# A hybrid encoder layer: tokens transposed before they are modulated

## What is computed

```
mod = silu(c) @ ada_w + ada_b                      # six rows of 1024 per group
sh1, sc1, g1, sh2, sc2, g2 = split(mod, 6)
h = rms_norm(x, norm1_g) * (1 + sc1) + sh1
z = h @ w_in                                       # q, k, v and the inputs of the recurrence
x = x + g1 * (concat[attention(q,k,v), rwkv7(z)] @ w_out)
h = rms_norm(x, norm2_g) * (1 + sc2) + sh2
x = x + g2 * experts(h)                            # top-1 group, top-2 experts
y = rms_norm(x, final_g)
```

## Time and profile before

| | |
|---|---|
| time, median of 3 runs | 1817.06 us (1814.21 to 1818.36) |
| the profiled execution | 1818.64 us, span 1816.9 us |
| PE busy | 1437.8 us (79%) |
| DVE, ACT, POOL busy | 623.9, 464.4, 297.5 us |
| moved | 321.22 MB, mean 177 GB/s |

### The profile page before, as it was taken

The page is one execution under the profiler, slowest core; times in us unless marked ns, Lnnn a source line. Parts: engine busy times, 40 slices in busy tenths (PEclk is TensorE's granted clock), DMA queues, the critical chain, the costliest instruction groups (busy, mean ns, idle before and its releaser), DMA issues. The chain is left out here.

```text
span 1816.9 us, 22753 instructions
## 1 busy us (share of the span) xinstructions
PE 1437.8 (79%) x8896; PEld 878.3 (48%) x8896; DVE 623.9 (34%) x1044; ACT 464.4 (26%) x1072; POOL 297.5 (16%) x278
## 2 busy tenths in 40 slices
PE   5799999996629999999989689719877777777750
PEld 1445456654217777777767335405443434343420
DVE  0500044331756666666667632320000000000006
ACT  1201124432224455544546211101100000000003
POOL 0000023220562222122230510030000000000002
PEclk9799999998759999999999789759989998989995
DMA  6535441111341000100000372169999999999975
GB/s 226 180 121 186 152 138 47 47 36 50 112 167 36 19 19 22 33 18 19 19 1 2 109 261 85 69 245 371 376 380 376 386 378 386 378 385 377 385 284 194
DMA packets 161374, 321.22 MB, mean 177 GB/s; under 512 B 12544, under 2 KB 37248, under 8 KB 160908
## 3 DMA queue, kind: packets, MB, share of 16 engines
q1 hardware_dynamic: 150636, 295.42, 45.6%
q0 software_dynamic: 4672, 14.69, 2.7%
q10 hardware_dynamic: 5984, 9.97, 1.5%
HBM read 288.05 MB, written 32.00 MB: 176 GB/s over the span
## 5 line engine op out<-in xcount | busy, mean ns | idle before, releaser
L1207 PE MATMUL bank<-arena 128*128 128x128 f16 (+6 forms) x3696 | 434.7, 272 | 68.4 <-DMA arena<-direction_scratch 29.8
L1207 PEld LDWEIGHTS bank<-arena 128*128 128x128 f16 (+1 forms) x3696 | 336.6, 138 | 164.9 <-issue 99.0
L1857 PE MATMUL bank<-arena 128*64 128x256 f32 x2048 | 268.1, 422 | 100.6 <-DMA arena<-in_exp_w 63.8
L1857 PEld LDWEIGHTS bank<-arena 128*64 128x64 f32 x2048 | 165.9, 152 | 214.4 <-issue 88.4
L610 PE MATMUL bank<-arena 128*128 128x512 f32 x368 | 167.0, 601 | 0.7 <-ACT arena L359 0.7
L1043 ACT CAST arena<-bank 128x384 f16<-128x384 f32 x360 | 158.5, 482 | 15.9 <-PE bank L1207 11.1
L1823 DVE TENSOR_TENSOR arena<-bank,arena 128x256 f32<-128x256 f32 x32 | 13.6, 426 | 374.1 <-PE bank L1857 374.1
L1163 DVE CAST arena<-bank 128x384 f16<-128x384 f32 x216 | 116.8, 556 | 64.6 <-PE bank L1207 62.9
L1875 PE MATMUL bank<-arena 128*64 128x512 f32 x512 | 116.9, 598 | 19.1 <-ACT arena L1796 19.1
L347 POOL TENSOR_SCALAR arena<-arena 128x256 f32<-128x256 f32 (+1 forms) x64 | 51.9, 821 | 354.2 <-DVE arena L538 354.2
L610 PEld LDWEIGHTS bank<-arena 128*128 128x128 f32 x368 | 66.8, 189 | 85.2 <-issue 83.3
(11 more groups left out here) (238 smaller groups left out, 1422.6 us busy)
## 6 DMA issues: line engine op xcount, KB each, us to landing
arena<-in_exp_w SPq DMA_DIRECT2D x96, 2048.0 KB, 21.0
arena<-in_ada_w SPq DMA_DIRECT2D x12, 2048.0 KB
arena<-in_w_in SPq DMA_DIRECT2D x23, 512.0 KB, 4.3
direction_scratch<-arena SPq DMA_DIRECT2D x6, 1536.0 KB, 5.5
arena<-direction_scratch SPq DMA_DIRECT2D x12, 768.0 KB, 4.6
slot_out<-arena ACTq DMA_DIRECT2D x64, 128.0 KB, 5.7
slot_out<-arena SPq DMA_DIRECT2D x1, 6144.0 KB
arena<-in_x_sample SPq DMA_DIRECT2D x8, 512.0 KB, 4.8
```

The lines of the kernel that those rows point to most:

```text
L1207: return nc.tensor.matmul(out, lhsT, r, start=start, stop=True, skip_group_check=True)
L1857: ins = nc.tensor.matmul(bank[b + 2 * c.s][BLK * n:BLK * n + BLK, 0:HALF], xT[c.s][:, j, :], slot[c.w][:, j, n * HALF:(n + 1) * HALF], sta ...
```

## The change

Tiles of x are only normalised (one DVE product with the reciprocal root) before they are transposed. Shift and scale are not spread over partitions; instead `mod_columns` turns each chunk of modp into columns, one value per feature on the partition of that feature, by four small matmuls, and DVE copies them to mcol. Then each transposed block is scaled and shifted in place with per-partition scalars, blocks 0, 1, 4, 5 by DVE and 2, 3, 6, 7 by ACT. Chunks come in the order 2, 3, 0, 1 (scale first). PE interleaves the transposes of the tiles with the chunks. The transposes alternate between two pairs of PSUM banks, x has four buffers. The first loads are x(0), identity, eps and x(1), ahead of the first chunk; the gain comes as a column, not broadcast; ada_b for the first four chunks comes in one load. project(0) comes ahead of the values. Cut to its core:

```diff
+        n1c = take(KD)
+        mcol = take(4 * KD).rearrange("p (m k g) -> p m k g", m=2, g=2)
...
+        NXB = 4
...
-        xb = [take(D) for _ in range(2)]
+        xb = [take(D) for _ in range(NXB)]
         hb = [take(D) for _ in range(2)]
-        rows = take(4 * D).rearrange("p (g m d) -> p g m d", g=2, m=2)
-        n1_row = take(D)
+        assert top[0] <= base5 + P // 2 + 5 * W + 3 * NT * W
+        adab4 = catT[:, 0:4, :].rearrange("p c t -> p (c t)")[:, 0:4 * 512]
...
-        ring = [("ada", c) for c in range(WV)] + [("wv", 0)] + [("ada", c) for c in range(WV, NCHUNK)]
+        ring = [("ada", c) for c in (2, 3, 0, 1)] + [("wv", 0)] + [("ada", c) for c in range(WV, NCHUNK)]
...
-            early = [(sel, A["c_sel"]), (ident, A["c_ident"]), (eps, A["c_eps"]), (mu[:, :, 0:2], A["mu"]),
-                     (n1_row, A["norm1_g"][0].partition_broadcast(P))]
...
             def x(t):
-                if t >= 2:
-                    sp.wait_ge(sem("x_used"), t - 1)
-                sp.dma_start(xb[t % 2], x_tile[t]).then_inc(sem(f"x_in{t % 2}"), 16)
+                if t >= NXB:
+                    sp.wait_ge(sem("x_used"), t - NXB + 1)
+                sp.dma_start(xb[t % NXB], x_tile[t]).then_inc(sem(f"x_in{t % NXB}"), 16)
+            x(0)
+            sp.dma_start(ident, A["c_ident"]).then_inc(sem("consts_in"), 16)
+            sp.dma_start(eps, A["c_eps"]).then_inc(sem("consts_in"), 16)
+            x(1)
             wide(0)
-            for dst, src in early:
-                sp.dma_start(dst, src).then_inc(sem("consts_in"), 16)
-            x(0)
-            x(1)
...
-                wide(r)
-            for t in range(2, NT):
-                x(t)
+            sp.dma_start(sel, A["c_sel"]).then_inc(sem("sel_in"), 16)
+            sp.dma_start(adab4[0:1, :], A["ada_b"][0:1, 0:4 * 512]).then_inc(sem("sel_in"), 16)
+            sp.dma_start(n1c, A["n1_cols"]).then_inc(sem("cols_in"), 16)
+            sp.dma_start(mu[:, :, 0:2], A["mu"]).then_inc(sem("cols_in"), 16)
+            x(2)
+            x(3)
+            wide(1)
+            x(4)
+            x(5)
+            wide(2)
+            win(0)
+            wide(3)
             wide(4)
-            for i in range(NWIN):
+            for i in range(1, NWIN):
...
                 act.wait_ge(sem("mod_mm"), i + 1)
-                nc.scalar.copy(modp[:, i * 512:(i + 1) * 512], bank[i % 2]).then_inc(sem("mod_ready"), 1)
-            for i in range(4):
-                mod(i)
+                c = i if i >= WV else ring[i][1]
+                nc.scalar.copy(modp[:, c * 512:(c + 1) * 512], bank[i % 2]).then_inc(sem("mod_ready"), 1)
...
             def rms(t):
-                act.wait_ge(sem(f"x_in{t % 2}"), 16 * (t // 2 + 1))
+                act.wait_ge(sem(f"x_in{t % NXB}"), 16 * (t // NXB + 1))
                 if t:
                     own.wait(own.n)
-                own.link(nc.scalar.activation(sq1, xb[t % 2], ACT.Square, scale=1.0 / 32.0, accum_out=stat[:, t, 0:1]))
+                own.link(nc.scalar.activation(sq1, xb[t % NXB], ACT.Square, scale=1.0 / 32.0, accum_out=stat[:, t, 0:1]))
                 own.done(nc.scalar.activation(stat[:, t, 1:2], stat[:, t, 0:1], ACT.Sqrt, bias=eps[:, 0:1]))
...
+            def hT_evac(t):
+                act.wait_ge(sem("hT_mm"), 2 * t + 1)
+                nc.scalar.copy(hT_half[0][:, :, t * P:(t + 1) * P], bank[2 + 2 * (t % 2)].rearrange("p (k c) -> p k c", k=4)).then_inc(sem("hT_act"), 1)
+            def modulate(k):
+                act.wait_ge(sem("cols_ready"), k // 4 + 3)
+                for g, (lo, hi) in enumerate(((0, T_S), (T_S, TOK))):
+                    nc.scalar.activation(hTk[k][:, lo:hi], hTk[k][:, lo:hi], ACT.Identity, bias=mcol[:, 0, k, g:g + 1],
+                                         scale=mcol[:, 1, k, g:g + 1]).then_inc(sem("h_act"), 1)
             rms(0)
...
-                act.dma_start(v_dram[t * P:(t + 1) * P, :], zs[t % 2][:, 0:W]).then_inc(sem(f"v_out{t % 2}"), 16)
+            hT_evac(0)
+            rms(2)
+            hT_evac(1)
+            rms(3)
+            mod(0)
+            hT_evac(2)
+            rms(4)
+            hT_evac(3)
+            rms(5)
+            mod(1)
+            hT_evac(4)
+            hT_evac(5)
+            mod(2)
+            act.wait_ge(sem("hT_act"), NT)
+            act.wait_ge(sem("hT_dve"), NT)
+            modulate(2)
+            modulate(3)
+            mod(3)
+            modulate(6)
+            modulate(7)
+            def values_out():
+                for t in range(NT):
+                    act.wait_ge(sem("v_mm"), t + 1)
+                    if t >= 2:
+                        act.wait_ge(sem(f"v_out{t % 2}"), 16 * (t // 2))
+                    nc.scalar.copy(zs[t % 2][:, 0:W], bank[2 + t % 2]).then_inc(sem("v_ready"), 1)
+                    act.wait_ge(sem("v_ready"), t + 1)
...
+                if i == 0:
+                    values_out()
...
-                ins = nc.vector.scalar_tensor_tensor(hb[t % 2], xb[t % 2], stat[:, t, 2:3], rows[:, group(t), 1, :], ALU.mult, ALU.mult)
-                ins.then_inc(sem("x_used"), 1)
-                dve.wait_ge(sem("x_used"), t + 1)
-                nc.vector.tensor_tensor(hb[t % 2], hb[t % 2], rows[:, group(t), 0, :], ALU.add).then_inc(sem("h_ready"), 1)
+                nc.vector.tensor_scalar(hb[t % 2], xb[t % NXB], stat[:, t, 2:3], None, ALU.mult).then_inc(sem("x_used"), 1)
...
+            def columns(r):
+                ks = slice(4 * (r % 2), 4 * (r % 2) + 4)
+                src = bank[6 + r % 2][:, 0:8].rearrange("p (k g) -> p k g", g=2)
+                dve.wait_ge(sem("cols_mm"), r + 1)
+                if r < 2:
+                    ins = nc.vector.scalar_tensor_tensor(mcol[:, 1, ks, :], src, 1.0, n1c[:, ks].unsqueeze(2).to_broadcast([P, 4, 2]), ALU.add, ALU.mult)
+                else:
+                    ins = nc.vector.tensor_copy(mcol[:, 0, ks, :], src)
+                ins.then_inc(sem("cols_ready"), 1)
+            def modulate(k):
+                for g, (lo, hi) in enumerate(((0, T_S), (T_S, TOK))):
+                    nc.vector.tensor_scalar(hTk[k][:, lo:hi], hTk[k][:, lo:hi], mcol[:, 1, k, g:g + 1], mcol[:, 0, k, g:g + 1],
+                                            ALU.mult, ALU.add).then_inc(sem("h_dve"), 1)
+            columns(0)
+            columns(1)
+            columns(2)
+            dve.wait_ge(sem("hT_act"), NT)
+            dve.wait_ge(sem("hT_dve"), NT)
+            dve.wait_ge(sem("cols_ready"), 3)
+            modulate(0)
+            modulate(1)
+            columns(3)
+            dve.wait_ge(sem("cols_ready"), 4)
+            modulate(4)
+            modulate(5)
...
+            def first_mod(r):
+                if r >= 2:
+                    pe.wait_ge(sem("mod_ready"), r - 1)
+                c = ring[r][1]
+                nc.tensor.matmul(bank[r % 2][0:32, :], sel[0:1, 2, 0:32], adab4[0:1, c * 512:(c + 1) * 512], start=True, stop=False)
+                pe.wait_ge(sem(f"wide_in{r % 2}"), 32 * (r // 2 + 1))
+                for k in range(2):
+                    for q in range(4):
+                        ins = nc.tensor.matmul(bank[r % 2][32 * q:32 * q + 32, :], siluT[:, 2 * q + k, :], adaw[r % 2][:, 2 * q + k, :],
+                                               start=(k == 0 and q > 0), stop=(k == 1), tile_position=(0, 32 * q))
+                ins.then_inc(sem("mod_mm"), 1)
+            def mod_columns(r):
+                c = ring[r][1]
+                pe.wait_ge(sem("mod_ready"), r + 1)
+                if r >= 2:
+                    pe.wait_ge(sem("cols_ready"), r - 1)
+                for j in range(4):
+                    ins = nc.tensor.matmul(bank[6 + r % 2][:, 2 * j:2 * j + 2], modp[:, c * 512 + j * P:c * 512 + (j + 1) * P], sel[:, 0:2, 0],
+                                           start=True, stop=True)
+                ins.then_inc(sem("cols_mm"), 1)
...
+            def x_T(t):
+                pe.wait_ge(sem("x_used"), t + 1)
+                for hf in range(2):
+                    if t >= 2:
+                        pe.wait_ge(sem("hT_act" if hf == 0 else "hT_dve"), t - 1)
+                    for k in range(4):
+                        ins = nc.tensor.transpose(bank[2 + 2 * (t % 2) + hf][:, k * P:(k + 1) * P], hb[t % 2][:, (hf * 4 + k) * P:(hf * 4 + k + 1) * P], ident)
+                    ins.then_inc(sem("hT_mm"), 1)
...
+            x_T(0)
+            x_T(1)
...
+            pe.wait_ge(sem("sel_in"), 32)
+            first_mod(0)
+            x_T(2)
+            x_T(3)
+            mod_columns(0)
+            first_mod(1)
+            x_T(4)
+            x_T(5)
+            mod_columns(1)
+            first_mod(2)
+            mod_columns(2)
+            first_mod(3)
+            mod_columns(3)
             pe.wait_ge(sem("hT_act"), NT)
             pe.wait_ge(sem("hT_dve"), NT)
...
+            pe.wait_ge(sem("cols_ready"), 4)
+            def modulated(k):
```

(26 more changed lines are left out.)

62 lines of the change are left out of this document (7 added, 55 removed).

## The result

The changed kernel takes 1787.64 us in the median of 4 runs (1787.18 to 1789.91), the kernel before 1815.89 us. The ratio is 0.9842 with a 95% interval of 0.9826 to 0.9858: 28.7 us less by the ratio, 28.3 by the medians. The forecast was 1794 us, a gain of 23.3, with a range of 1783 to 1799. Sign and place were right; the gain was 5 us larger than the forecast's, and the sum that led to it had wrong terms of opposite sign.

The account below looks back on a forecast made before the run. PE's own work bounds the kernel, so only time before its dense work can be won: 74.4 - 50.6 (PE's list at half clock) - 0.5 (slow start) = 23.3 us gain, forecast 1794 us, range 1783 to 1799.

Parts of the forecast that it names:

- The bound: Phase 1: PE's own work sets the time from the first projection; only the time before it, 74.38 us, can be won.
- The first tile: Start of the kernel: x(0) lands at about 4.7 us, scaling takes 0.7, first transposes start at 9.2.
- By the rows it stays at 1.2 GHz: PE's list before the dense work: all at half clock, project(0) starting at 50.6 us, not near 41.
- Chunk 0: First modulation chunk: operands landed at about 12.8 us, 5.3 us of PE at half speed, ending at 18.1.
- The loads have 3.6 to 7 us of slack: Chunk loads before the dense work: at half clock PE sets the pace; chunk 3's weights land at 37, needed at 44.
- rival A: Before the dense work: clock rises, loads then set the pace, start 40.5, gain 34 us, 1783 us; chance 0.14.
- B: Loads before the dense work: late transfers behind mu's small pieces, start 54 to 58, 1797 to 1802 us; chance 0.09.
- C: Dense work: clock stays at 1.2 GHz as project(0) stops for each block's modulation; slower, up to 1843 us; chance 0.02.
- D: Token tiles: order of loads leaves them as late as before, so no change; chance 0.02.
- mu and the held queue: Loads of x(2), x(3): mu's 8-byte pieces hold queues and SP, x(2) lands at 15.8, PE loses 0.8 us.
- The modulation: Scaling and shifting blocks before project(0): hidden under chunk 3 and project(0)'s first matmuls; without that cover some 2 us.
- The slow start of the dense work: Start of project(0): first microseconds at 1.2 GHz in either version, charged 0.5 us more than before.

Follow-up runs that it names:

- the second pair of profiles: The kernel before and the changed kernel, each profiled and timed once more with no edit: medians 1815.08 and 1786.75 us.
- e1: The changed kernel with the load of mu and its two DVE operations moved behind chunk 4 and the modulation: 1784.69 us.
- e6: e1 with win(0), the first 0.5 MB block of w_in, loaded behind chunk 3 instead of ahead of it: 1783.97 us.
- e8: e6 with the selector and the row of ada_b loaded ahead of chunk 0 instead of behind it: 1782.12 us.
- e2: The changed kernel with the values projection again ahead of project(0), waiting for all eight modulated blocks: 1793.22 us.
- e3: The kernel before with the Silu waiting for c_cols alone, mu and broadcast gain loaded late, chunk 1 ahead of x(0) and x(1): 1809.28 us.
- e5: The changed kernel with interleaving undone: four chunks with columns first, then six token tiles; x(4), x(5) loaded behind the value weights: 1800.27 us.
- e7: e6 with four filler matmuls of 384 columns while PE waits for chunk 3: 1784.80 us.

## Why the prediction was right, and where its steps were wrong

The time came out inside the range and the start of the dense work near the forecast (47.68 for 50.6), but partly by another mechanism: the prediction had PE's own list at half clock set that start, and the runs show the last load setting it, ahead of a list that was faster than reckoned.

*The bound.* Right: all that changed is when PE's dense work begins, and what is won there stays. From 53.5 us on PE has no gap to 197, and in the second pair of profiles the differences at the phase starts stay within 0.6 us of each other (28.3 to 28.9; 27.8 at the end). In the first pair they go from 25.7 to 31.2, of which 3.2 are the step in phase 4.

*The first tile.* Right within 0.7 us: the first transposes at 9.91 for 9.2, and 9.2 to 9.5 in five of the other profiles of the changed kernel and its variants (10.1 and 10.3 in two). The scaling took 0.75 us for the 0.7 extrapolated from L1085.

*"By the rows it stays at 1.2 GHz."* Wrong. In the changed kernel's first profile chunk 2 and the columns 1 and 2 ran at full clock; in the second, chunk 2, the columns 0 to 2 and the transposes of the last two tiles did. The list was not slow in every part, though its kinds of work were the ones I had called slow. Rows 8 had warned: the same L1636 had run at either level. So had L579 in rows 2: 16 matmuls of 128x512 took 10.34 us, where L610 takes 7.03 for as many. The trace shows a spread of durations in it, and twice the count after 47 us as before 46:

```profile
L579 PE MATMUL bank<-arena x16: 592/697/1222, 41.1 to 50.9; 128*128 128x512 f32 x16
45.00:46.00 1.00, 1.00 (x2) 0.32 (x2) 0.63 (x1) 0.29 (x1) 0.00 (x0) 1.00 0.00 0
47.00:48.00 1.00, 1.00 (x4) 0.30 (x2) 0.66 (x2) 0.00 (x0) 0.00 (x0) 1.00 0.00 0
```

So the clock rose inside the prefix of the kernel before as well, near 47 us, and was down again by 54. I took the 10.34 for a price at half clock when I bounded mod_columns by it. The rule of the Trainium skill that I had weighed (TensorE: Matmul & The Clock Gate, "Why this matters for your kernels": keep the engine busy and the clock is released) was nearer; the trace agrees with it at 33 us, when the clock rose after PE had gone from 20.17 on through transposes, tiny and narrow matmuls without a pause. It is no full account either: by 40.6 the clock was down again, after 7 us in which no pause of PE was longer than 0.71 us. Against the sum, PE's pieces took 6.1 us less in the first profile, nearly all of it in those that found the clock up; had this been all, the dense work would have begun at 44.5.

*Chunk 0.* I had its operands landed at 12.8; PE waited for the selector and the bias row until 14.65 in the first profile, 13.96 in the second. That is 1.9 and 1.2 us of PE's list, in the first profile the largest price of a load. It is not mu's: in e1 and e6, without mu, chunk 0 began at 13.96 and 14.67. With those two loads put first (e8) the wait was gone, but the first transposes came at 10.25, and chunk 0 began at 13.82. What held the two loads up isn't shown.

*"The loads have 3.6 to 7 us of slack."* Wrong, and this took part of that back: PE waited 0.67 us for chunk 3 in the first profile and 3.15 in the second. I put its landing at 37, from the 7.9 us of issue to use in the kernel before; it landed at 40.4 to 41.1 in three profiles, 10.1 us after its issue in one and 12.8 (27.81 to 40.61) in another. The 7.9 us belonged to a transfer with empty queues; here chunk 2 and win(0) were ahead of it. The right sum is that of all bytes: rival A had the right form (loads set the pace), but without the hole that mu made. With 373 GB/s from 15 us on, x(2) to x(5), chunks 1 to 3 and win(0), 8.9 MB, are 24 us, and 15 + 24 is 39, plus landing. e1 closed the hole and chunk 3 moved by 2.5 to 3 us, e6 and e8 took 0.5 MB out of its way and it moved by 1 to 2.

*The rivals.* A's place of the bound came true and its clock in part; its 40.5 was 7 us too early. B's transfers did come late, but the price was charged against a list of PE that was shorter than reckoned, so the start stayed below 50.6. C did not happen: project(0) was slow for 5.6 us and no longer, and no block kept it waiting. D neither: the last transposes ended at 33.9.

*mu and the held queue.* I had the mechanism, but its size was off: SP was held 8.80 us, not the 5.14 of the old row, and x(2) was used at 17.57 (I had it landed at 15.8). Its price to PE ahead of x_T(2) was 1.4 for 0.8 in the first profile and nothing in the second; to chunk 3 it was some 3 us, which I had not charged at all.

*mod_columns* took 1.71 to 1.87 us at the slow level and 0.95 to 1.05 at the fast one, for 1.8 and 1.0. *The modulation* is hidden under project(0)'s start: PE went on at 47.68 while ACT worked from 47.51 to 50.01. Without that cover it costs 2.6 us at the start of the dense work, where I had 2 (e2), and 0.9 to 2.0 at the mark.

*The slow start of the dense work.* I charged 0.5 us more than before; project(0) ran slow until 53.3, 5.6 us, where the values had been slow for 3.1, or 5.2 in the second profile of the kernel before. It cost 1.4 in the one pair and nothing in the other.

So 74.4 - 50.6 - 0.5 became 74.4 - 47.7 - 1.4 = 25.3, or 28.6 with the second profiles, 27 on the mean. The step that failed is the sum to 50.6: PE's own list was shorter than at half clock, and the last load, not the list, set its end. In the first profile the sum closes as 50.6 - 6.1 (shorter pieces of PE) + 1.9 (chunk 0's operands) + 0.6 (x(2)) + 0.7 (chunk 3) = 47.7. That it came so near is in part luck: errors of 6.1 and 3.2 us stood against each other.

Where the gain comes from is known in part. Earlier constants, with chunk 1's load first, bring about 7 us (e3). Putting the token work under the loads is 9 us in the start, 6 at the mark and 13 in the median (e5). Projecting queries first is 1 to 2 us at the mark and 5.6 in the median (e2). What the work that is gone (row matmuls, two-operand scaling) brings was not tested by itself. These parts were undone one at a time, so they need not add up.

**Left open.** What exactly brings the clock up or down within the first 50 us was not settled: the executions of near relatives had different patterns, and two kinds of filler did not pay. The medians of e5 and e2 lie above the changed kernel's by 7 and 4 to 5 us more than their profiles show at the mark, and only a part of that was found. Differences below 3 us between e1, e6, e7 and e8 are not told apart by the times; only the dates of chunk 3 in the profiles are.

## What to carry to other kernels

When a stage is a list of waits for loads, don't price a load by its time in an empty queue. Add the bytes that stand ahead of it, and check by that sum when the last one can land. A transfer in pieces of 8 bytes can cost the queues and the issuing engine far more than its size: this one (15 KB) held SP for 8 us and cost the last of four 2 MB loads 3 us; it belongs behind everything that is waited for. Work that doesn't need the late operand (here normalising and transposing, which commute with a per-feature scale) goes under the load of that operand; that was worth 9 us in the start of the dense work here, and 6 to 13 in the time.

When the same number of equal instructions takes two different times in one trace, as L579 and L610 did, don't take either as the price before it is known at which clock they ran.

## What was not expected of the hardware

- The granted clock in two executions of one kernel was not the same. In phase 4, which has the same instructions each time, it fell in some executions (492 us from its first transfer to the next stage's, 494.9 in e2) and not in others (489 us). Two profiles of the kernel before differed by 3 us there and by 2 us in the first 130, without any edit.
- The clock rose behind narrow matmuls and transposes (at 33 us in the changed kernel, project(0) not having begun), and it was down in the same kinds of work at 16.5 to 33 and, by their durations, in the kernel before.
- A single 15 KB load in 8-byte pieces brought the rate down to 95 GB/s over 3 us (12 to 15 us), against 373 GB/s from 15 us on, and 386 from 9 us on in e1, where it was moved away.
